# The start of the projection stage in a decoder trunk on one core: order of the squares, banks of the turned tokens, order of the weight rounding, dummy matmuls

## The reference

```python
h = concatenate([meta, x])                       # 528 x 1024
u = rmsnorm(h, g_attn)                           # y = h * rsqrt(mean(h*h) + 1e-6) * g
proj = u @ w_in                                  # 1024 x 2216
fq, fk, fv, ff, cq, ckv, kr = split(proj)        # 512, 512, 512, 8, 384, 256, 32 columns
fq, fk = rmsnorm per head of 64
log_f = log_sigmoid(ff + b_f); cum = cumsum(log_f)
# then: 8 forgetting-attention heads on fq, fk, fv, cum; 8 latent-attention heads on
# rmsnorm(cq), rmsnorm(ckv), kr; output projection and residual; a mixture of experts
# (32 experts of 3 MB of weights each, two per token); residual
```

## Time and profile before

| | before |
|---|---|
| median of three timed executions | 687.35 us |
| profiled execution, own time | 685.2 us |
| its span | 683.6 us |
| its mean granted TensorE clock | 0.94 |
| projection stage (up to the last turned ckv unit) | about 0 to 156 us |
| from the first gathered expert on, DMA nearly full | about 427 us to the end |

### The profile page before, as it was taken

One profiled execution on the slowest core, in us unless ns is written; L12 is line 12 of the kernel. 1 busy time (PEld: TensorE's weight loads), 2 busy tenths in 40 slices (PEclk: granted clock), 3 DMA queues, 4 the chain that ended last, 5 costly groups with the idle time before them and its releaser, 6 DMA issues.

```text
span 683.6 us, 9020 instructions
## 1 busy us (share of the span) xinstructions
PE 591.6 (87%) x3389; PEld 381.2 (56%) x3389; DVE 232.1 (34%) x539; ACT 214.8 (31%) x410; POOL 156.8 (23%) x233
## 2 busy tenths in 40 slices
PE   6699999998996997999899957999997888888850
PEld 6577778885663554666455534555544455445520
DVE  2554144224566476363455541111111111111105
ACT  6626415243454341544244421121121111111110
POOL 8000001111236811343200111323322222122110
PEclk9899999999999998999999977999999999999985
DMA  8900000008500001000590185999999999999929
GB/s 264 388 16 0 1 1 0 1 7 306 206 1 0 1 0 63 1 0 1 210 373 31 40 337 202 375 387 384 393 384 398 395 397 392 394 390 394 379 88 357
DMA packets 35811, 136.01 MB, mean 199 GB/s; under 512 B 8809, under 2 KB 10905, under 8 KB 26817
## 3 DMA queue, kind: packets, MB, share of 16 engines
q1 hardware_dynamic: 29536, 124.92, 47.9%
q0 software_dynamic: 5664, 8.55, 4.0%
q10 hardware_dynamic: 576, 2.10, 0.8%
HBM read 131.28 MB, written 12.65 MB: 211 GB/s over the span
## 4 chain that ended last, share of the span: by engine, by line
PE 66%; SPq 9%; DVE 9%; DMA 9%; issue 4%; ACT 3%; POOL 0%; POOLq 0%; DVEq 0%
PE ps L1696 14%; PE ps L2003 12%; PE ps L1767 7%; PE ps L1858 6%; PE ps L1847 6%; PE ps L2030 5%; DMA w<-in_w 4%; SPq L613 3%; SPq L612 3%; PE ps L1911 3%; SPq L619 3%; PE ps L1963 2%; DMA yg<-y_rows 2%; PE ps L1823 2%; PE ps L1660 1%
## 5 line engine op out<-in xcount | busy, mean ns | idle before, releaser
L2003 PE MATMUL ps<-w,xt 128*64 128x256 f32 x1024 | 129.9, 411 | 26.7 <-issue 21.2
L2003 PEld LDWEIGHTS ps<-w,xt 128*64 128x64 f32 x1024 | 85.5, 148 | 81.2 <-issue 52.4
L1565 DVE TENSOR_TENSOR xt<-ps,g_ffn_c 128x512 f32<-128x512 f32 x32 | 22.1, 692 | 214.1 <-PE ps L1963 214.1
L2030 PE MATMUL ps<-w,hT 128*64 128x512 f32 x256 | 61.8, 604 | 0.0
L827 POOL DMA_INDIRECT xg<-u_rows,idx x32 | 30.6, 957 | 127.2 <-PE ps L1963 115.9
L1121 ACT ACTIVATE hsb<-ps 128x256 f32<-128x256 f32 x32 | 12.3, 383 | 149.1 <-PE ps L2003 149.1
L817 POOL DMA_INDIRECT y_rows<-yh,idy x32 | 32.4, 1011 | 79.2 <-ACT yh L1139 79.2
L1767 PE MATMUL ps<-w_oa,mixT 128*128 128x512 f32 x96 | 44.4, 599 | 2.0 <-issue 2.0
L1858 PE MATMUL ps<-probT,vals 128*128 128x512 f32 (+4 forms) x160 | 42.6, 410 | 0.0
L1847 PE MATMUL ps<-qT,kT 68*128 68x400 f32 (+9 forms) x160 | 42.2, 408 | 0.1
L753 POOL TENSOR_SCALAR_AFFINE_SELECT probT<-probT 128x128 f32<-128x128 f32 (+2 forms) x80 | 20.2, 271 | 87.4 <-ACT probT L1044 86.9
(11 more groups left out here) (298 smaller groups left out, 901.3 us busy)
## 6 DMA issues: line engine op xcount, KB each, us to landing
w<-in_w SPq DMA_DIRECT2D x96, 1024.0 KB
yg<-y_rows SPq DMA_DIRECT2D x4, 1024.0 KB, 8.0
w_oa<-in_w_o SPq DMA_DIRECT2D x1, 3072.0 KB, 17.5
x<-in_x SPq DMA_DIRECT2D x4, 512.0 KB, 5.3
w_in_v<-in_w_in SPq DMA_DIRECT2D x1, 2048.0 KB, 10.3
w_in_k<-in_w_in SPq DMA_DIRECT2D x1, 2048.0 KB, 15.4
w_in_q<-in_w_in SPq DMA_DIRECT2D x1, 2048.0 KB, 21.5
u_rows<-u2n ACTq DMA_DIRECT2D x4, 512.0 KB, 4.4
```

What stands on the lines that cost most here:

```text
L2003: ins = pe.matmul(ps[j * slots:(j + 1) * slots, 2 + b, 0:F], xt[b][:, k, :], w13[s][:, j, k, :], start=(k == 0), stop=(k == DK - 1))
L2030: ins = pe.matmul(ps[q * slots:(q + 1) * slots, 6 + b, :], hT[b][:, m, :], w2s[s][:, m, q * 512:(q + 1) * 512], start=(m == 0), stop=(m == ...
```

## The change

In `projection_plan`, a unit's turn is no longer placed behind a gather but behind the next projection. Each of the five token tiles gets its own `scale_x` and a pair of banks from X_BANKS; only the last one waits (for `u_low(0)`). ACT does all five squares, with `u_high(0)` behind that of j=1, then `u_high(1)`, `u_high(2)`, `w_high("ffcq")`, `u_high(3)`, `u_high(4)`, `w_high("v")`. DVE makes all five `scale_x` first, then the low parts, with `w_low("ffcq")` ahead of `u_end` and `u_low` of j=3 on. TensorE starts with eight float32 matmuls of `ident` with itself into bank 7. Units of ffcq wait for as many `u_low` as their banks need. ACT gets one more wait ahead of the squares of ffcq 2 and 3 and ckv units.

```diff
@@ projection_plan
+    pending = []
     for n, u in enumerate(units):
         steps.append(("gather" if in_groups(u) else "project", u))
-        if n >= 1 and turned(units[n - 1]):
-            steps.append(("turn", units[n - 1]))
+        if not in_groups(u):
+            steps += [("turn", v) for v in pending]
+            pending = []
+        if turned(u):
+            pending.append(u)
...
-    steps.append(("turn", units[-1]))
+    steps += [("turn", v) for v in pending]
@@ build
-        scale_x = [place(f"scale_x{b}", [P, P], F32, r_p + 6144 + 512 * b) for b in range(2)]
+        scale_x = [place(f"scale_x{j}", [P, P], F32, r_p + 3072 + 512 * j) for j in range(NT + 1)]
@@ turn_freed
-            if u[0] == "x":
+            if turns[n][0] == "x":
+                if n == len(TOKEN_TILES) - 1:
+                    eng.wait_ge(u_lo_made, 1)
+            elif u[0] == "x":
                 eng.wait_ge(u_lo_made, n - 1)
...
+        X_BANKS = [4, 6, 0, 2, 4]
@@ block.scalar
-                if j in (1, 2):
-                    u_high(j - 1)
+                if j == 1:
+                    u_high(0)
+            u_high(1)
             u_high(2)
+            w_high("ffcq")
             u_high(3)
             u_high(4)
-            w_high("ffcq")
             w_high("v")
...
+                    if stage_no[u] >= 2:
+                        act.wait_ge(staged_done, stage_no[u] - 1)
@@ block.vector
-                if j >= 2:
-
-                    dve.wait_ge(turned, j - 1)
...
-            norm_tokens(0)
             for j in range(len(TOKEN_TILES)):
-                if j + 1 < len(TOKEN_TILES):
-                    norm_tokens(j + 1)
+                norm_tokens(j)
+            for j in range(len(TOKEN_TILES)):
+                if j == 3:
+                    w_low("ffcq")
                 if j in (0, 1, len(TOKEN_TILES) - 1):
...
                 u_low(j)
-            w_low("ffcq")
@@ block.tensor
             pe.wait_ge(ident_made, 1)
+            for _ in range(8):
+                pe.matmul(ps[:, 7, 0:P], ident[:, :], ident[:, :], start=True, stop=True)
...
                 if b == "ffcq":
 
-                    pe.wait_ge(u_lo_made, TOKEN_TILES.index(t) + 1)
+                    pe.wait_ge(u_lo_made, max(TOKEN_TILES.index(t) + 1, 3 + n // 2))
```

More of the change, by code:

```diff
@@ L530, in turn_freed @@
                 eng.wait_ge(turn_dve, sum(by_dve(v) for v in turns[:n - 1]))
+        X_BANKS = [4, 6, 0, 2, 4]
         def turned_x(j):
             r = rows(TOKEN_TILES[j])
-            b0 = 4 + 2 * (j % 2)
+            b0 = X_BANKS[j]
             return ps[:, b0:b0 + 2, 0:DK // 2 * r].rearrange("p q (k n) -> p q k n", n=r)
@@ L1214, in norm_tokens @@
                 dve.wait_ge(roots_made, j + 1)
-                if j >= 2:
-                    dve.wait_ge(turned, j - 1)
                 step(dve.reciprocal(rinv[j % 2][0:r, 0:1], root[0][0:r, j:j + 1]))
-                dve.tensor_scalar(scale_x[j % 2][0:r, 0:r], ident[0:r, 0:r], rinv[j % 2][0:r, 0:1], None, ALU.mult
+                dve.tensor_scalar(scale_x[j][0:r, 0:r], ident[0:r, 0:r], rinv[j % 2][0:r, 0:1], None, ALU.mult
                                   ).then_inc(scale_made, 1)
@@ L1660, in turn @@
                         ins = pe.matmul(ps[:, b0 + q, kk * r:(kk + 1) * r], src[:, k * P:(k + 1) * P],
-                                        scale_x[j % 2][0:r, 0:r], start=True, stop=True)
+                                        scale_x[j][0:r, 0:r], start=True, stop=True)
                     ins.then_inc(turned, 1)
```

## The result

The changed kernel takes 680.27 us (median of four executions, 678.60 to 680.96) against 687.72 us for the kernel before in the same comparison (687.33 to 688.15): ratio 0.9893, 95 % interval 0.9865 to 0.9920. That is a gain of 7.45 us; the forecast was 8.95 us and 678.4 us. The profiled execution took 679.61 us, its span is 678.0 us, 5.6 us less than before.

What follows compares the result with a forecast made beforehand. The prediction took a stream of expert weights to bound the late stage and a chain of waits the beginning. Its terms, 5.6 + 1.6 + 1.0 + 1.45 - 0.7 = 8.95 us, gave a median of 678.4 us, range 676.2 to 681.8.

Steps and rivals of the forecast that it cites:

- A: Start up to the first full ffcq tile: low part of the weights done at 22.2 instead of 27.87, gain 5.6 us.
- B: First full ffcq tile: the clock holds over a pause of 2.6 us, gain 1.6 us; bounds 1.6 and a loss of 1.7.
- The walk: Step-by-step timing of the start: slow dummies, third turn ends 15.5, weights land 16.5, low part done 22.2.
- all three signs: At the start: clock 0.50 in the first full tile, token passes at 0.127 us, ACT waiting for `w_in_ffcq`.
- The rival of working dummies: At the start: fast pace from about 5 us, gain 9.75 us, time 677.6 us; chance 0.12.
- first rival: Clock falls before or in the first full tile: gain 7.35 down to 5.65 us, 680.0 to 681.7 us; chance 0.24.
- C: Turn of ffcq 3 moved behind v 0, filling TensorE's stall after the v gather: gain 1.0 us, bounds 0.7 and 1.2.
- D: Turn of q 3 moved behind ckv 0, filling the stall after the ckv gather: gain 1.45 us, bounds 0.8 and 1.5.
- E: Around the cumulative sum: the clock may fall inside its narrow passes, estimated loss 0.7 us, bounds 0 and 2.8.
- The forecast's own range: Whole kernel's time: 676.6 to 680.2 us, from a start gain of 4.4 to 6.4 and a cumulative-sum loss of 0 to 1.8.
- mark of 147.2: End of the projection: the last turned ckv unit expected at about 147.2 us instead of 155.7.
- everything displaced alike: Behind the last ckv turn: nothing late stands at a fixed time, so all of it moves by the earlier gain.

Runs made afterwards that it cites:

- e5_split_load: The changed kernel with the ffcq weights loaded in two halves, each with its own semaphore; ratio to the kernel before 0.9904.
- e4_bridge: The changed kernel with dummy matmuls filling the pause ahead of the first full ffcq tile; 680.54 us, ratio to the kernel before 0.9890.
- e1_plan_only: The kernel before with only the new order of turns (ffcq 3 behind v 0, q 3 behind ckv 0); ratio to before 0.9971.
- e3_no_dummies: The changed kernel without the eight dummy matmuls at the start; 681.10 us, ratio to the kernel before 0.9898.
- e9_late_weights: The changed kernel with the ffcq weights' transfer held back until the small vectors are in; 683.52 us, ratio to the kernel before 0.9946.
- e7_split_bridge: The changed kernel with the ffcq weights loaded in halves and fewer dummy matmuls filling the pause before the first full tile; ratio to before 0.9869.
- e2_start_only: The changed kernel with the old order of turns, so the new beginning alone; ratio to the kernel before 0.9904.

## Why the prediction was right, and where it was off

The sign, the range and the main term held: 680.27 us lies in 676.2 to 681.8, and A came out at 5.63 us for 5.6. Of the 8.95 us forecast 7.19 stand at the stage end, and nearly all that is missing is term B. By its steps:

**A was right in size and wrong in its path.** The walk had the dummies fail, the third turn end at 15.5 and the weights land at 16.5, 0.1 us ahead of their need. In the profile the dummies worked, and the weights landed at 17.17 (13.9 us from the issue instead of the 13.2 of the earlier trace rows). DVE's last low part then came at 22.25 for 22.2, by another way. It wasn't luck alone: with the slow start (e5_split_load) the steps are those of the walk, meta turn 3.59 us for 3.5, third turn at 15.33 for 15.5, first full tile at 21.98. All the same, all three signs that the prediction had named for being wrong were seen: a clock of 0.50 in the first full tile, fast token passes, and a wait of ACT for `w_in_ffcq` (3.47 us). The last two nearly cancel in A, a walk 0.8 us shorter and a landing 0.7 us later, and that is luck. Two knots at nearly the same time make the sum robust and each part's removal worthless: without dummies 22.09, with halves 21.98.

**The rival of working dummies** came true in its condition and not in its price. It let A be 6.4 by a landing at 16.5; with 17.17 the row of high and low parts behind it ends at 22.25. The rule of the Trainium skill named there ("TensorE: Matmul & The Clock Gate", Part 1) agrees with three of the eight kernels with eight dummies: their meta turn ran at full pace right behind the dummies. In the other five the meta turn was still slow; the same section says that the moment of the rise varies from run to run, which these eight profiles show too.

**B is the step that failed.** The forecast took 1.6 us of gain, because a pause of 2.6 us lay nearer to one of 1.9 that had kept the clock. In the profile the token turns ended at 15.4, not at 19.6 (they ran at full pace), so the pause was 6.9 us long, as long as before. The faster start lengthened the pause that then lowered the clock. The measured -0.08 is the first rival's case: with B at 0 it gave a gain of 7.35 us and 680.0 us, and the stage end shows 7.19. That the median is 680.27 is nearer than these sums can be held to, for the part behind the stage scatters by 3.6 us (below). e4_bridge shows the 1.6 us to be there once the pause is filled. With a slow start the pause is short, as in the walk, and the clock fell all the same: in e5_split_load the turns ended at 18.9, the first full tile began at 21.98 and took 7.26 us, 1.1 us more than before. So the step fails there too: the clock didn't hold over a pause of 3.1 us, near the 2.6 of the walk.

**C and D** were measured at 1.11 and 1.64 for 1.0 and 1.45. The turns behind a full product cost less than where they had to wait, 0.33 for 0.52 and 0.87 for 1.04. The forecast left the first out, and took the second the wrong way round: it held 0.87 for a little more than the turn had cost in the stall.

**E** was -1.11 for an estimate of -0.7, within its bounds. The mechanism is that of the forecast in its first half: the clock fell at 73.7 instead of 82.55, now inside the passes, which took 5.02 us (71.18 to 76.20) for 4.00 before (77.84 to 81.84). The gather and k 0 behind them cost nearly the same, 8.75 us (76.20 to 84.95) for 8.66 (81.84 to 90.50, the wait for DVE included), since the low clock had lain on k 0 before as well. In e1_plan_only, where the fall came later in the passes, it was the other way round: 4.25 and 9.59 us.

**The sums.** The forecast's own range doesn't follow from its terms: with A at 4.4 and E at -1.8 the gain is 6.65 us and the time 680.7, not 680.2, and E had been bounded by 2.8 just before. Its mark of 147.2 for the last turned ckv unit doesn't follow either, 155.87 - 8.95 is 146.9. The range for 8 in 10 is wide enough to hold both.

**Behind the stage** the forecast had everything displaced alike. In the profiled execution 1.6 us were lost between the last ckv turn and the first scores: 161.69 - 155.87 = 5.82 us before, 156.13 - 148.68 = 7.45 after, where the clock was low in between:

```profile
152.30:155.60 3.30, 3.30 (x15) 1.72 (x14) 1.75 (x4) 0.37 (x1) 0.00 (x0) 0.50 0.73 101
```

This isn't a property of the change: e3_no_dummies and e9_late_weights, with the same code there, take 5.8 us for this stretch, e7_split_bridge 7.5. It is why the span shrank by 5.6 us and not by the 7.19 of the stage. That the median fell by 7.45 is another matter: the profiled execution of the kernel before lay 2.5 us under its median (685.2 and 687.72), that of the changed kernel only 0.7. For the profiled kernels the time behind the stage end is between 527.7 and 531.3 us, the least in the kernel before, and that scatter of 3.6 us is half of the whole gain.

## What to carry to other kernels

Before moving a step forward, write down what it will wait for next, with the landing times of its transfers: here a landing with 5.4 us of slack became the knot, and from then on splitting the transfer or warming the clock at the start had nothing to gain. A faster stage ahead of a fixed landing makes TensorE's pause longer, and the clock that falls in it takes back what the dense work behind gains; fill the pause up to the dense work, not the start of the program, and break long rows of narrow passes into pieces between dense ones. Where single executions scatter by as much as an edit is worth, compare marks in the chain, and use the median only for the sum.

## What was not expected of the hardware

The same eight dummies, at the same times from 1.72 us, were followed by a fast meta turn (1.95 to 2.15 us) in three kernels and a slow one (3.59 us) in five. The clock's changes don't stand at fixed points of the program: in the changed kernel it fell at 73.7 and 152.2 us, in e2_start_only, with nearly the same work, the passes from 72.45 all ran at full pace. Up to the first rise the rows of the granted clock say 1.00 although the passes run at half pace (0.237 us instead of 0.127 each), so that at a program's start the pace has to be read, not the clock. And the landing of the first block of weights, with the queue's order untouched, came at 16.5 us in the kernel before and at 17.0 to 17.2 us in five others that issue it at 3.26 us in one piece, among them e1_plan_only, whose beginning is that of the kernel before.
